# A decoder layer: gate and up projections with the weights as the stationary operand

## The reference, cut to what matters

```
h = rmsnorm(x, pre_ffn_norm)
f = (silu(h @ w_gate) * (h @ w_up)) @ w_down        # 1024 -> 2816 -> 1024
x = x + rmsnorm(f, post_ffn_norm)
```

## Time and profile before

| | us |
|---|---|
| median of 3 runs | 318.73 (318.72 to 318.75) |
| span of the profiled execution, first to last instruction | 316.7 |
| TensorE products busy | 307.7, 97% |
| DVE busy | 180.9, 57% |
| ACT busy | 150.9, 48% |
| instructions executed | 4110, of them 1432 products and 1432 weight loads |

### The profile page before, as it was taken

The page is one execution under the profiler, slowest core; times in us unless marked ns, Lnnn a source line. Parts: engine busy times, 40 slices in busy tenths (PEclk is TensorE's granted clock), DMA queues, the critical chain, the costliest instruction groups (busy, mean ns, idle before and its releaser), DMA issues.

```text
span 316.7 us, 4110 instructions
## 1 busy us (share of the span) xinstructions
PE 307.7 (97%) x1432; PEld 247.1 (78%) x1432; DVE 180.9 (57%) x255; ACT 150.9 (48%) x248; POOL 24.6 (8%) x27
## 2 busy tenths in 40 slices
PE   6999999999999999999999999999999999999992
PEld 3788867778888888778888888888888888888881
DVE  2858447675467497899555555544444454551426
ACT  5887654436409164676444444444433333340322
POOL 2020045000002000540000000000000000000001
PEclk9999999999999999999999999999999999999998
DMA  7999994405451553279955555555655655400003
GB/s 212 405 406 378 411 395 138 148 26 184 150 155 46 199 155 112 71 220 314 340 179 174 179 193 185 167 178 191 199 199 199 199 197 192 141 0 0 0 2 132
DMA packets 17518, 58.35 MB, mean 184 GB/s; under 512 B 1998, under 2 KB 2518, under 8 KB 17505
## 3 DMA queue, kind: packets, MB, share of 16 engines
q1 hardware_dynamic: 17136, 57.06, 52.3%
q0 software_dynamic: 368, 1.11, 1.0%
HBM read 57.10 MB, written 1.06 MB: 184 GB/s over the span
## 4 chain that ended last, share of the span: by engine, by line
PE 90%; DVE 4%; POOL 2%; DMA 2%; ACT 1%; issue 0%; SPq 0%; DVEq 0%
PE bank L942 26%; PE bank L944 26%; PE bank L943 25%; PE bank L952 4%; DMA raw<-in_w_in 2%; PE bank L969 1%; POOL xs L442 1%; PE bank L1043 1%; PE bank L1041 1%; PE bank L973 1%; PE bank L977 1%; DVE d_lo L867 1%; DVE res L933 1%; DVE w_lo L860 1%; PE bank L1075 1%; DVE res L927 1%
## 5 line engine op out<-in xcount | busy, mean ns | idle before, releaser
L942 PE MATMUL bank<-w_hi,a_hi 128*128 128x512 f32 x256 | 101.7, 397 | 0.0
L944 PE MATMUL bank<-w_hi,a_lo 128*128 128x512 f32 x256 | 100.1, 391 | 0.0
L943 PE MATMUL bank<-w_lo,a_hi 128*128 128x512 f32 x256 | 99.7, 390 | 0.0
L944 PEld LDWEIGHTS bank<-w_hi,a_lo 128*128 128x128 f32 x256 | 48.0, 188 | 10.5
L942 PEld LDWEIGHTS bank<-w_hi,a_hi 128*128 128x128 f32 x256 | 48.1, 188 | 10.3 <-issue 0.7
L608 ACT ACTIVATE sil<-bank,rstd 128x256 f32<-128x256 f32 x22 | 10.4, 473 | 95.8 <-PE bank L944 93.4
L943 PEld LDWEIGHTS bank<-w_lo,a_hi 128*128 128x128 f32 x256 | 48.1, 188 | 9.8
L860 DVE TENSOR_TENSOR w_lo<-raw,w_hi 128x1024 fp32r<-128x1024 f32 x40 | 49.5, 1276 | 6.5 <-ACT w_hi L593 6.5
L875 DVE SCALAR_TENSOR_TENSOR hid<-bank,rstd,sil 128x256 f32<-128x256 f32 x22 | 10.6, 484 | 74.3 <-ACT sil L608 74.3
L672 DVE TENSOR_TENSOR w_lo<-raw,w_hi 128x1024 fp32r<-128x1024 f32 x32 | 40.3, 1281 | 17.9 <-ACT w_hi L456 17.9
L593 ACT ACTIVATE w_hi<-raw 128x1024 fp32r<-128x1024 f32 x40 | 40.4, 1057 | 0.0
(11 more groups left out here) (116 smaller groups left out, 299.2 us busy)
## 6 DMA issues: line engine op xcount, KB each, us to landing
raw<-in_w_gu SPq DMA_DIRECT2D x44, 512.0 KB, 4.5
raw<-in_w_dn SPq DMA_DIRECT2D x22, 512.0 KB, 4.7
raw<-in_w_in SPq DMA_DIRECT2D x20, 512.0 KB, 9.1
raw<-in_w_out SPq DMA_DIRECT2D x8, 512.0 KB, 3.2
raw<-in_w_in SPq DMA_DIRECT2D x8, 256.0 KB, 5.5
xs<-in_x SPq DMA_DIRECT2D x2, 512.0 KB, 8.2
bias<-bias_row POOLq DMA_DIRECT2D x1, 1024.0 KB, 9.8
out<-res SPq DMA_DIRECT2D x4, 256.0 KB, 2.0
```

The lines of the kernel that those rows point to most:

```text
L942: pe.matmul(acc, hi, wh, start=first, stop=False)
L943: pe.matmul(acc, hi, wl, start=False, stop=False)
L944: return pe.matmul(acc, lo, wh, start=False, stop=last)
```

## The change

The first group of 256 inner columns stays as it is (row form). From inner column 256 on the roles are swapped: an inner block b of 128 columns (b from 2 to 21, FIRST = 2, NB = 22) has its 128 x 128 weight blocks as the stationary operand and all 256 tokens move. `turned_block(b, up)` is 8 k x 3 = 24 products of 256 columns, once for gate and once for up, 48 per block, into a bank whose partitions are inner columns. The result is already in the form that the down projection wants, so the transposes of hid are gone for these blocks.

Since the token is now in the free dimension, r can't be a per-partition scale of ACT. It is needed as a row, the same on all 128 partitions: ACT makes `diag`, the identity scaled by r, for both tiles, and `factor_row` is one product of ones x diag (plain fp32), which DVE copies to `r_row`. DVE then makes z = gate * r_row (`z_block`), ACT sil = silu(z), DVE hid = up * sil, ACT h_hi, DVE h_lo, all 128 x 256. The r on up is left out; the whole of f is scaled by it at the end instead: ACT's squares take a scale `rf` per row, and res becomes (f * r) * gain.

The down projection runs by blocks of 128 inner columns, 12 products of 512 columns each as before (2 t x 2 c x 3), 264 in all. A weight unit of gate and up now holds the eight k blocks of one inner block's gate, or of its up. Sizes and count of the loads are the same. All engine loops are written out. Shortened:

```diff
+FFN = [("gu", 2 * b + i) for b in (FIRST,) for i in range(2)] + [("dn", b) for b in range(FIRST)]
+for _b in range(FIRST + 1, NB):
+    FFN += [("gu", 2 * _b), ("gu", 2 * _b + 1), ("dn", _b - 1)]
+FFN += [("dn", NB - 1)]
...
 # ACT
+            for b in range(FIRST, NB):
+                nxt = LEAD_FFN + 3 * (b - FIRST)
+                silu_block(b)
+                for i in range(nxt, min(nxt + 2, len(FFN))):
+                    hi_ffn(i)
+                h_hi_block(b)
+                for i in range(nxt + 2, min(nxt + 3, len(FFN))):
+                    hi_ffn(i)
...
 # DVE
-            lo_gu(1, 1, 1)
-            hidden(0, 0)
-            lo_gu(1, 2, 1)
-            lo_gu(1, 3, 1)
+            lo_ffn(1)
+            lo_ffn(2)
+            hidden_rows(0)
+            lo_ffn(3)
...
 # TensorE
+            def factor_row():
+                pe.wait_ge(ones_ready, 1)
+                pe.wait_ge(diag_ready, NT)
+                pe.wait_ge(x1_ready, 2)
+                pe.matmul(pr_row[:, 0, 0:S], ones[:, :], diag[:, :, :].rearrange("p t i -> p (t i)"),
+                          start=True, stop=True).then_inc(row_done, 1)
...
+                for k in range(NK):
+                    wh, wl = w_hi[:, slot, k * P:(k + 1) * P], w_lo[:, slot, k * P:(k + 1) * P]
+                    pe.matmul(acc, wh, a_hi[:, k, :], start=(k == 0), stop=False)
+                    pe.matmul(acc, wh, a_lo[:, k, :], start=False, stop=False)
+                    ins = pe.matmul(acc, wl, a_hi[:, k, :], start=False, stop=(k == NK - 1))
+                ins.then_inc(w_used, 1)
...
-            gate_up(0, 1, 0)
-            turn_hidden(0, 0)
-            group(1, 1)
-            with pe.Fori(2, NF - 2, 2) as g:
-                group(g, 2)
-                group(g + 1, 3)
-            group(NF - 1, NF - 1)
-            turn_hidden(NF - 1, 1)
-            down(NF - 1, 0, NF - 1, last=True)
-            down(NF - 1, 1, NF - 1, last=True)
+            gate_up_rows(1)
+            turn_rows(0)
+            turned_block(FIRST, 0)
+            turn_rows(1)
+            factor_row()
+            turned_block(FIRST, 1)
+            for b in range(FIRST):
+                down_block(b)
+            for b in range(FIRST + 1, NB):
+                turned_block(b, 0)
+                turned_block(b, 1)
+                if b < NB - 1:
+                    down_block(b - 1)
+            for t in range(NT):
+                for c in range(2):
+                    down(NB - 2, t, c)
+                    down(NB - 1, t, c).then_inc(f_done, 1)
```

More of the change, by code:

```diff
@@ L66 @@
 DRING = 4
+HBUF = 4
 HALVED = 4
@@ L458, in _, with squares @@
             squared = [0]
-            def squares(what, t, c, src):
+            def squares(what, t, c, src, scale=1.0 / math.sqrt(D)):
                 if squared[0]:
@@ L618, in group, with h_hi_rows @@
[L618 to L632 removed]
+            def h_hi_rows(t):
+                act.wait_ge(h_turned[t], 1)
+                act.activation(h_hi[:, 0:FIRST, t * P:(t + 1) * P],
+                               pt[:, t, 0:FG].rearrange("p (b i) -> p b i", i=P),
+                               ACT.Copy).then_inc(hhi_ready[t], 1)
@@ L639, in _ @@
-            silu(0, 0)
-            hi_gu(1, 3, 1)
+            hi_ffn(2)
+            diagonal(0)
+            silu_rows(0)
+            hi_ffn(3)
             x1_squares(1)
-            hi_dn(0, 0, 0)
-            wait_factor(act, X1_, 1)
-            silu(0, 1)
-            h_hi_part(0, 0)
-            hi_dn(0, 1, 0)
-            group(1, 1)
-            with act.Fori(2, NF - 2, 2) as g:
-                group(g, 2)
-                group(g + 1, 3)
-            group(NF - 1, NF - 1, more=False)
@@ L897, in _, with h_lo_block @@
+            def h_lo_block(b):
+                dve.wait_ge(hbhi_ready, b - FIRST + 1)
+                dve.tensor_tensor(h_lo[:, b % HBUF, :], hid[:, b % 2, :], h_hi[:, b % HBUF, :].bitcast(F32),
+                                  ALU.subtract).then_inc(hblo_ready, 1)
             residual(0)
             a_lo_part(1, 0)
-            lo_gu(1, 0, 1)
+            lo_ffn(0)
             a_lo_part(1, 1)
@@ new lines, in down @@
+            def down(b, t, c):
+                n = unit_n("dn", b)
+                if b < FIRST:
+                    pe.wait_ge(hlo_ready[t], 1)
+                else:
+                    pe.wait_ge(hblo_ready, b - FIRST + 1)
+                if b == 0:
+                    pe.wait_ge(x1_ready, 2 * t + 2)
+                    pe.wait_ge(row_ready, 1)
+                pe.wait_ge(lo_ready, n + 1)
+                ins = product(pf[t][:, c, :], h_hi[:, b % HBUF, tile(t)], h_lo[:, b % HBUF, tile(t)],
+                              d_hi[:, b % DRING, c * CW:(c + 1) * CW], d_lo[:, b % DRING, c * CW:(c + 1) * CW],
+                              first=(b == 0), last=(b == NB - 1))
+                return ins
```

360 lines of the change are left out of this document (181 added, 179 removed).

## The result

| | us, median (runs) | ratio to before, 95% interval |
|---|---|---|
| before | 318.74 (318.72 to 318.75, 4 runs) | |
| after | 325.31 (323.6 to 326.54, 4 runs) | 1.0195 [1.0164, 1.0226] |

The changed kernel is 2% **slower**. The forecast was 323.0, with a range of 314.8 to 326.6. Unlike before, its runs differ among themselves by 3 us, and the time follows the mean granted clock: 323.6 us at 0.999, 325.25 at 0.993, 325.37 at 0.989, 326.54 at 0.985. The last is the profiled one; its span is 324.7 us.

The account below looks back on a forecast made before the run. TensorE's own rate was taken as the bound. From the second transposes on 4.2 us more, plus 0.1 at the end, took 316.7 to 321.0; 2.0 from profiled span to run median gave 323.0 us, range 314.8 to 326.6.

Parts of the forecast that it names:

- Price of a 256-column product: Gate and up on TensorE: 0.120 us per 256-column product, a fixed extra of 0.0133 us paid per product; chance 0.50.
- rivals 1: Gate and up products: the extra is proportional to columns, 0.1133 us each, 6.3 us less, total 316.7; chance 0.17.
- 2 (the load floor of 0.111): Gate and up products: the extra vanishes, only the weight load limits, 8.4 us less, total 314.6; chance 0.13.
- 3 (0.124): Gate and up products: load floor and extra add up, 3.7 us more, total 326.7; chance 0.13.
- Transposes: Feed-forward on TensorE: 40 of 44 transposes of hid leave, 0.11 us each, 4.4 us less.
- Down products 0.229: Down projection on TensorE: 264 products at 0.229 us, the middle of 0.2267 to 0.231, together 60.5 us.
- The sum from the second transposes on: From second transposes to the last stream's end: 174.3 us against 170.1 before, 4.2 us more.
- The last wait: Behind the last gate/up block, TensorE waits for hid, h_hi and h_lo: 0.85 us, between 0.7 and 1.1.
- Idle time ahead of the second transposes: Start of the stage: TensorE idles about 2 us; the second transposes stay at 140.7, give or take half a microsecond.
- Rival 4: TensorE is fed too slowly, or idling lowers its clock, costing 1.5 us; a feed limit, over 328; 0.07 with rival 5.
- rival 5: Product weight loads: those for equal stationary operands are dropped, one in three; under 2 in 100.
- The output work: At the very end, ACT's squares take a factor per row: 0.1 us more on the path.

Follow-up runs that it names:

- experiment 1: The changed kernel with rows of unread products of several widths and number formats behind its last one, to time their starts; 338.15 us in its one run.
- experiment 2: The kernel before with each 512-column gate and up product cut into two of 256 from the second group on; 323.47 us, ratio 1.0152.
- experiment 4: The changed kernel with 11 unread 512-column products in TensorE's gap ahead of the second transposes; 323.77 us, ratio 1.0157.
- experiment 6: The changed kernel with only the last down products reordered, 6 instead of 3 ahead of the one needing h_lo; 324.65 us, ratio 1.0191.
- experiment 7: Two runs on the changed kernel: POOL's memset of ones moved behind its first DMAs, 325.76 us; DVE's hid(0) put ahead of down unit 0's split, 324.34 us.

## Why the prediction came out as it did

- **Price of a 256-column product: right.** 0.120 us where 0.120 was chosen, and as argued the extra over the columns is paid once per product (experiment 1), independently of the roles (experiment 2). That it is the load that makes it was argued too, and is not shown. The rivals 1 (0.1133), 2 (the load floor of 0.111) and 3 (0.124) fall. The floor exists, at 0.111, but lies under 256 columns' own price. One reading behind the choice doesn't hold: the distances are not the same while DVE is busy and after it. From 186.70 to 189.22 us there are 11 in 2.52 us, 0.229 each. But over the whole feed-forward part of the kernel before the longer distances are the first 18 or so behind a pair of transposes (0.230 to 0.232 on average, with DVE busy or idle); further on they are 0.2267 either way. So the conclusion, that no other engine makes the extra, stands, by this and by experiment 1.
- **Transposes: right**, 0.109 against 0.11 us, with what they cost the down products behind them.
- **Down products 0.229: right.**
- **The sum from the second transposes on, 174.3 us: right at full clock.** In the kernel of experiment 4 they start at 141.56 and the last stream ends at 315.85: 174.3. In the profiled run of the changed kernel, 141.76 to 318.66, it is 176.9.
- **The last wait, 0.85: right**, 0.89 (experiment 6).
- **Idle time ahead of the second transposes: mechanism right, size short.** About 2 us were forecast, 2.9 were there. The forecast left the transposes at 140.7 since "DVE and ACT have the same steps there in the same order"; that step failed. Ahead of it DVE's unit had moved in front of hid, to the start of POOL's additions, and those took 4.18 instead of 3.50 us (experiment 7). The prediction had allowed for a slower unit on DVE there (up to 1.8 us) and not for slower additions. The other 0.4 us came from the start of the kernel, and how much of them is the change's isn't known.
- **Rival 4, the clock: it came true**, at 2.6 us in the profiled run where 1.5 was estimated, and in one run of four hardly at all. It was a case beside the forecast, with 7 in 100 together with rival 5; it belonged into the sum. From 143.31 to 147.58 us, 20 distances at 0.2135 instead of 0.120 are 1.9; the transposes, the factor row and the first product are the rest.
- **The output work, 0.1: too small.** It is 0.3: not only ACT's squares (0.60 to 0.69) but DVE's last step, which now takes a factor per row as well (0.68 to 0.75, twice on the path).

For the profiled run: 321.0 forecast, + 1.0 for the later transposes, + 2.6 for the clock, + 0.2 for the output work, is 324.8; the span is 324.7. For the fastest run, at clock 0.999, the forecast of 323.0 is 0.6 short.

The median, 325.31, lies in the stated range of 314.8 to 326.6, but above the forecast's own, 322.0 to 324.3. The wide range reached so far up only for half of rival 3, a price of 0.124 that no run shows, and it left rival 4, which came true, outside. That the number fell inside is in part luck.

## What to carry to other kernels

Where TensorE is the bound, count the products as well as the columns: swapping the roles of the operands to save 40 transposes (4.4 us) cost 480 more products with 0.013 us of fixed price each (6.2 us), and gave the transposes back with interest. If roles are swapped, keep the moving side at 512 columns (here by laying the high and low parts side by side) and give TensorE other work ahead of each new dependency; with both, the last down products reordered and the widths grouped, the same idea was 0.6% faster than before instead of 2% slower. A gap of 2.3 to 2.9 us on TensorE at full clock cost its length and, in most runs, a stretch at half rate behind it: filler products in it were cheaper than leaving it empty.

## What the runs showed of the hardware that was not expected

- The fixed price is that of fp32r with a 128-wide stationary operand: 0.013 us; bf16 and plain fp32 have 0.003. With a stationary operand 64 wide it was 0.007 at 256 columns, but at 512 it was not smaller (mean 0.229 us, between 0.225 and 0.236). What causes it isn't settled.
- The first five 512-column products behind a run of 256-column ones start 0.228 to 0.236 us apart instead of 0.227.
- Two additions on POOL take 3.50 to 3.56 us with one neighbouring step on DVE and 4.18 with the two exchanged; DVE's two units then take 2 x 1.2 instead of 3.4 to 3.6 together. In these profiles a unit that DVE started just ahead of an addition kept to 1.2 us, and one started during an addition took up to 2.3.
- The fall of the granted clock behind the gap lasts 6.8 us in some profiles and 3.4 in others, and not by the gap's length: 6.8 behind 2.90 us (the changed kernel), 3.4 behind 2.88 (experiment 6) and 2.27 (experiment 7), no fall behind 2.89 (experiment 1). The four runs of the changed kernel, at mean clocks of 0.985 to 0.999, spread by 3 us.
